# Slot table of a mixture-of-experts layer summed by TensorE in PSUM, in place of ten scatters through memory

## The reference, cut to what matters

```
g_p, g_idx = top_k(softmax(x @ router_group_w + b), 1)          # 1 of 4 groups
e_p, e_idx = top_k(softmax(logits of the 8 experts there), 2)   # 2 of 8 experts
weights = g_p * e_p / sum(e_p)
hid = silu(x @ w_gate[e]) * (x @ w_up[e])                       # e: 1024 -> 256
out = sum over the 2 experts of weights[e] * (hid @ w_down[e])
```

## Time and profile before

| what | value |
|---|---|
| time, median of 3 runs (range) | 1311.78 us (1309.76 to 1312.71) |
| profiled execution: its time, its span | 1309.53 us, 1307.7 us |
| PE busy, DVE busy, ACT busy, POOL busy | 70%, 47%, 22%, 7% of the span |
| granted TensorE clock, mean | 0.789 of 2.4 GHz |
| HBM read, written | 181.74 MB, 19.36 MB |

### The profile page before, as it was taken

One profiled execution on the slowest core, in us unless ns is written; L12 is line 12 of the kernel. 1 busy time (PEld: TensorE's weight loads), 2 busy tenths in 40 slices (PEclk: granted clock), 3 DMA queues, 4 the chain that ended last, 5 costly groups with the idle time before them and its releaser, 6 DMA issues. The chain is left out here.

```text
span 1307.7 us, 15405 instructions
## 1 busy us (share of the span) xinstructions
PE 919.8 (70%) x5907; PEld 578.9 (44%) x5907; DVE 615.1 (47%) x1286; ACT 294.1 (22%) x499; POOL 89.3 (7%) x71
## 2 busy tenths in 40 slices
PE   1699988989368786776867659983047899697710
PEld 1365555666255665665756324452012344242300
DVE  2317999355568676786742432335601111010124
ACT  2230000323525244273211540101000111010102
POOL 0000000010010010100100000001311111111031
PEclk9889999989675575755756779985568999798965
DMA  9835511200110011101140730110359999989543
GB/s 334 291 153 210 196 55 57 75 9 17 17 26 9 10 25 17 26 1 18 25 164 3 276 163 33 49 49 19 147 232 381 394 421 419 377 340 398 193 156 145
DMA packets 72967, 193.72 MB, mean 148 GB/s; under 512 B 42629, under 2 KB 43023, under 8 KB 58687
## 3 DMA queue, kind: packets, MB, share of 16 engines
q1 hardware_dynamic: 64272, 174.05, 35.8%
q0 software_dynamic: 5840, 10.63, 2.1%
q10 hardware_dynamic: 2783, 8.06, 1.7%
HBM read 181.74 MB, written 19.36 MB: 154 GB/s over the span
## 5 line engine op out<-in xcount | busy, mean ns | idle before, releaser
L521 PE MATMUL bank<-arena 128*128 128x320 f32 x704 | 200.8, 445 | 14.3 <-DVE arena L413 6.1
L521 PEld LDWEIGHTS bank<-arena 128*128 128x128 f32 x704 | 135.3, 194 | 81.5 <-issue 30.0
L1998 PE MATMUL bank<-arena 128*64 128x512 f32 (+2 forms) x528 | 131.0, 668 | 34.7 <-DMA arena<-in_expert_w_up 33.6
L921 DVE SCALAR_TENSOR_TENSOR arena<-arena 128x655 f32<-128x655 f32 x116 | 104.7, 902 | 4.6 <-DVE arena L921 0.2
L1998 PEld LDWEIGHTS bank<-arena 128*64 128x64 f32 (+2 forms) x528 | 45.7, 151 | 118.3 <-issue 116.9
L1466 PE MATMUL bank<-arena 128*128 128x512 f32 x160 | 78.6, 655 | 11.6 <-issue 11.6
L2079 DVE TENSOR_TENSOR arena<-arena,bank 128x256 f32<-128x256 f32 x17 | 7.2, 422 | 161.6 <-ACT arena L2053 161.6
L2020 PE MATMUL bank<-arena 128*64 128x512 f32 (+2 forms) x264 | 62.4, 599 | 9.9 <-DVE arena L2082 9.9
L883 ACT ACTIVATE arena<-bank 64x128 f32<-64x128 f32 (+1 forms) x68 | 19.9, 292 | 170.7 <-PE bank L1256 169.4
L1466 PEld LDWEIGHTS bank<-arena 128*128 128x128 f32 x160 | 33.4, 211 | 54.2 <-issue 54.2
L1984 PE MATMUL bank<-arena 128*128 128x128 f32 x136 | 19.7, 290 | 52.9 <-DMA arena<-tokens_for_experts,arena 52.9
(11 more groups left out here) (309 smaller groups left out, 1440.9 us busy)
## 6 DMA issues: line engine op xcount, KB each, us to landing
arena<-in_expert_w_gate SPq DMA_DIRECT2D x33, 1024.0 KB, 14.4
arena<-in_expert_w_up SPq DMA_DIRECT2D x33, 1024.0 KB, 17.2
arena<-in_expert_w_down SPq DMA_DIRECT2D x33, 1024.0 KB, 18.3
arena<-in_ada_w SPq DMA_DIRECT2D x12, 2048.0 KB, 10.2
arena<-in_w_in SPq DMA_DIRECT2D x22, 512.0 KB, 3.7
arena<-expert_rows SPq DMA_DIRECT2D x10, 512.0 KB, 8.4
arena<-in_x_sample SPq DMA_DIRECT2D x8, 512.0 KB, 7.7
arena<-in_w_out SPq DMA_DIRECT2D x1, 4096.0 KB, 14.7
```

The lines of the kernel that those rows point to most:

```text
L521: mm = nc.tensor.matmul(psum[4 + 2 * (n % 2) + half][:, 0:HALF], wring[:, n % NWIN, k], hT[:, k, half * HALF:(half + 1) * HALF], start=(k ...
L921: chain(nc.vector.scalar_tensor_tensor(acc, src, w, acc, ALU.mult, ALU.add))
L1998: mm = nc.tensor.matmul(psum[2 + n % 2][r, :], xeT[:, n % 2, c, r], gu[:, :, c, :], start=(c == 0), stop=(c == KD - 1))
```

## The change

The table is made in PSUM. For each of the 10 columns DVE writes a one-hot of the row's lane (128 x 128, `lane_hot`) and a one-hot of its tile times its two values (128 x 74, `tile_val`), and PE sums the 10 products; DVE then turns the sums into token, output row and gate value in `tab`. The table is still stored to `slots`, behind everything, since the overflow rounds read a column of it there. The blank table, the 10 scatters and the read are gone.

The ranking is done with one expert per partition: PE brings the 32 counts to rows and columns of 32 partitions, DVE compares and looks the rank's first tile, lane offset and size up in a constant (`rank_rows`), and PE spreads three values per expert over all partitions and gives the experts in order of rank. `s_ids` is announced as soon as that is there. POOL's memset of `xe` no longer has a table write ahead of it. Constants for the one-hots (`late`, 261 columns) are loaded with the modulation rows. SP's load 4 waits for `s_ovst` alone.

```
@@ dve_route
-            chain(nc.vector.memset(initt[:, :, 2:4], 0.0))
-            chain.announce(nc.vector.memset(initt[:, :, 0:2].bitcast(I32), MISS), s_tinit0, 1)
...
+            for src, own, dst in ((iot, t32, krow), (lane0, kc, kcol)):
+                chain(nc.vector.tensor_scalar(own, src, float(FIXED_EXPERTS[1]), 2.0, ALU.is_equal, ALU.mult))
+                chain(nc.vector.scalar_tensor_tensor(own, src, float(FIXED_EXPERTS[0]), own, ALU.is_equal, ALU.add))
+                chain(nc.vector.scalar_tensor_tensor(dst, own, -65536.0, src, ALU.mult, ALU.subtract))
+            e_ = slice(0, 32)
+            dve.wait_ge(s_cnt, 1)
+            chain(nc.vector.scalar_tensor_tensor(key[e_], psum[4][e_, 0:32], 32.0, krow[e_], ALU.mult, ALU.add))
+            chain(nc.vector.scalar_tensor_tensor(kc[e_], psum[4][e_, 32:33], 32.0, kcol[e_], ALU.mult, ALU.add))
+            chain(nc.vector.tensor_scalar(gt[e_], key[e_], kc[e_], None, ALU.is_gt))
+            chain(nc.vector.tensor_reduce(rank[e_], gt[e_], AX_X, ALU.add))
+            chain(nc.vector.tensor_scalar(onehot[e_], iot[e_], rank[e_], None, ALU.is_equal))
...
-            chain(nc.vector.tensor_tensor(cmp_, key.unsqueeze(1).broadcast_to(w3), key.unsqueeze(2).broadcast_to(w3),
-                                          ALU.is_gt))
-            chain(nc.vector.tensor_reduce(rank, cmp_, AX_X, ALU.add))
...
+            dve.wait_ge(s_vec, 1)
+            chain.announce(nc.vector.tensor_copy(eid[0:1].bitcast(I32), psum[5][0:1, 96:128]), s_ids, 1)
+            chain(nc.vector.tensor_copy(vrow, psum[5][:, 0:96].rearrange("p (v e) -> p v e", e=32)))
...
+            chain(nc.vector.tensor_tensor(tile_hot, const("slot_row").unsqueeze(1).broadcast_to(st),
+                                          flat_tile.unsqueeze(2).broadcast_to(st), ALU.is_equal))
+            chain(nc.vector.tensor_tensor(tile_val, tile_hot.unsqueeze(2).broadcast_to(sv),
+                                          vals.unsqueeze(3).broadcast_to(sv), ALU.mult))
+            chain.announce(nc.vector.tensor_tensor(lane_hot, const("lane_row").unsqueeze(1).broadcast_to(sl),
+                                                   flat_lane.unsqueeze(2).broadcast_to(sl), ALU.is_equal), s_pos, 1)
+            dve.wait_ge(s_tabsum, 1)
...
+            chain.announce(nc.vector.tensor_copy(tab[:, :, 2], psum[7][:, NSLOT:2 * NSLOT]), s_tab, 1)
@@ pe_route
+            for i in range(TILES):
+                nc.tensor.matmul(psum[4][0:32, 0:32], ones[:, 0:32], both[:, i], start=(i == 0), stop=(i == TILES - 1))
+            for i in range(TILES):
+                mm = nc.tensor.matmul(psum[4][0:32, 32:34], both[:, i], ones[:, 0:2], start=(i == 0), stop=(i == TILES - 1))
+            mm.then_inc(s_cnt, 1)
...
+            pe.wait_ge(s_pos, 1)
+            for n in range(NLANE):
+                mm = nc.tensor.matmul(psum[7][:, 0:2 * NSLOT], lane_hot[:, n], tile_val[:, n].rearrange("p v s -> p (v s)"),
+                                      start=(n == 0), stop=(n == NLANE - 1))
+            mm.then_inc(s_tabsum, 1)
@@ pool_route, act_table
-            pool.wait_ge(s_tinit0, 1)
-            pool.dma_start(slots.rearrange("(p a) b -> p a b", p=P), initt.bitcast(I32)).then_inc(s_tinit, 16)
...
-            for n in range(NLANE):
-                pool.indirect_dma_start(out=slots, out_offset=At(ap=sloti[:, n:n + 1].bitcast(U32), axis=0),
-                                        in_=ent[:, n, :].bitcast(I32), in_offset=None).then_inc(s_scat, 16)
...
-            act.dma_start(tab.bitcast(I32), slots.rearrange("(p a) b -> p a b", p=P)).then_inc(s_tab, 16)
+            act.dma_start(slots.rearrange("(p a) b -> p a b", p=P), tab.bitcast(I32)).then_inc(s_slotst, 16)
```

More of the change, by code:

```diff
@@ L50 @@
 NPAR = _at
+CAP = P // 2
+NHOT, NPAIR, NQUAD = 6, 6, 3
+NTILE = NHOT + 1 + NPAIR + NQUAD + 1
+NOV = 20
+NSLOT = NTILE + NOV
+SECOND, COLD, FIXED = NHOT + NPAIR, NHOT + 2 * NPAIR, NEXP - 2
+FIXED_EXPERTS = (0, 16)
+MISS = 1 << 20
+ROWS = [(NTILE - 1, (FIXED, FIXED + 1))]
+_taken = {"S": 0, "P": 0, "Q": 0}
+for _kind in "PQPSSPSPSSQHPQP":
+    if _kind == "H":
+        ROWS += [(0, (0,)), (1, (0,))]
+        continue
+    _m = _taken[_kind]
+    _taken[_kind] += 1
+    ROWS.append({"S": (2 + _m, (1 + _m,)), "P": (NHOT + 1 + _m, (NHOT + _m, SECOND + _m)),
+                 "Q": (NHOT + 1 + NPAIR + _m, tuple(COLD + _m + NQUAD * j for j in range(4)))}[_kind])
 CONSTS = [("ident", 128), ("headones", 128), ("ones", 128), ("gmask", 128), ("scanmask", 512),
-          ("before", 128), ("expiota", 32), ("lanes", 8), ("ovi", 24), ("sel", 2)]
+          ("before", 128), ("expiota", 32), ("lanes", 8), ("ovi", 24), ("sel", 2),
+          ("lane_row", 128), ("slot_row", NSLOT), ("rank_rows", 96)]
 COFF = {}
@@ L120, in build @@
         keep = Region(0)
-        cst = keep.take(NCONST)
+        cst = keep.take(NKEEP)
         par = keep.take(NPAR)
@@ L1322, in build @@
         eid = regp.take(32)
+        late = regp.take(NCONST - NKEEP)
         regs = Region(ebuf[NB - 1], ebuf[1])
@@ L1713, in dve_route @@
             chain(nc.vector.reciprocal(t2, t2))
[L1714 to L1720, removed]
+            chain(nc.vector.tensor_copy(vals[:, 0:TILES, 1], t2))
+            chain(nc.vector.tensor_tensor(vals[:, TILES:NLANE, 1], t2, t3, ALU.mult))
+            chain(nc.vector.memset(tab, 0.0))
             dve.wait_ge(s_rank, 1)
@@ L1778, in dve_route @@
-            for k in range(2):
-                chain(nc.vector.tensor_copy(e2[:, k * TILES:(k + 1) * TILES, 0], tok))
-                ins_ = nc.vector.tensor_scalar(e2[:, k * TILES:(k + 1) * TILES, 1], tok, float(k * T), None, ALU.add)
-                if k == 0:
-                    chain(ins_)
-            chain.announce(ins_, s_ent, 1)
-            chain(nc.vector.tensor_tensor(cmp_, rank.unsqueeze(1).broadcast_to(w3), iot.unsqueeze(2).broadcast_to(w3),
-                                          ALU.is_equal))
@@ L1787, in dve_route @@
-            chain(nc.vector.tensor_tensor(cmp_, cmp_, iot.unsqueeze(1).broadcast_to(w3), ALU.mult))
-            chain(nc.vector.tensor_reduce(key, cmp_, AX_X, ALU.add))
-            chain.announce(nc.vector.tensor_copy(eid.bitcast(I32), key), s_ids, 1)
+            chain(nc.vector.tensor_scalar(big, sec, float(P + 1), None, ALU.is_ge))
+            chain(nc.vector.scalar_tensor_tensor(tl, dd, float(-P), isov, ALU.is_ge, ALU.subtract))
+            chain(nc.vector.tensor_tensor(tl, tl, big, ALU.mult))
@@ new lines, in dve_route @@
+            chain(nc.vector.scalar_tensor_tensor(dest, psum[7][:, 0:NSLOT], 1.0, blank, ALU.subtract, ALU.add))
+            chain(nc.vector.tensor_scalar(blank, dest, float(T), float(-T), ALU.is_ge, ALU.mult))
+            chain(nc.vector.tensor_tensor(blank, blank, dest, ALU.add))
+            ti = tab.bitcast(I32)
+            chain(nc.vector.tensor_copy(ti[:, :, 0], blank))
+            chain(nc.vector.tensor_copy(ti[:, :, 1], dest))
+            chain.announce(nc.vector.tensor_copy(tab[:, :, 2], psum[7][:, NSLOT:2 * NSLOT]), s_tab, 1)
@@ L2223, in _constants @@
     c["ovi"] = np.tile(np.arange(24), (P, 1))
+    c["lane_row"] = np.tile(np.arange(P), (P, 1))
+    c["slot_row"] = np.tile(np.arange(NSLOT), (P, 1))
+    first = np.zeros((3, NEXP))
+    for tile, ranks in reversed(ROWS):
+        rows = P // len(ranks)
+        for j, k in enumerate(ranks):
+            first[0, k], first[2, k] = tile, rows * sum(k in r for _, r in ROWS)
+            first[1, k] = first[2, k] + rows * j
+    c["rank_rows"] = np.tile(first.reshape(1, 96), (P, 1))
     c["sel"] = (i[:, None] % 32 == np.arange(2)[None]) * 1.0
```

132 lines of the change are left out of this document (61 added, 71 removed).

## The result

The changed kernel takes 1289.57 us (median of 4 runs, 1286.99 to 1292.88) against 1310.77 us (4 runs) of the kernel before: ratio 0.9849, 95% interval 0.9819 to 0.9878, that is 16 to 24 us less: under 2%, but clear of the scatter. Two later sets of the same kernel gave 0.9842 and 0.9838.

A forecast was written before the change was run, and what follows sets the result against it. Taken as bound by the slot table and the DVE chain ahead of PE's first tile. Steps summed to 23.8 us gained: 1309.5 to 1285.7 for the profiled execution, 1288.0 against the median of 1311.78; range 1285 to 1296.

The forecast's parts named there:

- What bounds: Slot table and the DVE chain ahead of it delay PE's first tile; the weight stream starts with that tile.
- Start of the routing: POOL's memset holds the first DVE tensor_scalar until 902.65; experts picked at 909.2 instead of 908.9, plus 0.3 us.
- DVE to the marks: DVE from expert pick to one-hot marks: 11.7 us removed, 10.25 added, net minus 1.5; marks ready at 928.7.
- Waits for PE inside it: Ten small counting matmuls take 1.2 us plus 0.2, hidden under six key steps to 0.1; at the bound DVE waits 3.2.
- The table: Ten PE matmuls, 20 records, take 4.4 us plus 0.2; DVE's reading 1.5; table at 934.8 instead of 952.7.
- The gather: First gather of token rows runs alone, taking 3.7 us instead of 9.59; bounds 2.6 and 9.6.
- Together: All steps up to PE's first tile: it starts at 939.4 instead of 963.23, a gain of 23.8 us.
- Downstream: Behind the first tile everything moves whole; load 5 comes 12 us behind it; load 4, if late, is late by 1 us.
- A contended gather: Rival: first gather still takes 9.6 us, or PE is at its upper bounds; gain 17.9, 1293.9 us; chance 0.15.
- The stream did not follow load 4: Rival claimed the weight stream follows load 4, not PE, so only 12.9 us are kept: 1299 us; chance 0.06.
- the case with more gain: Rival: late memset (1.3), gather 2.6 us (1.1), tile 0 at 2.4 GHz (7.3 for 8.81 us); gain 27.7, 1284; chance 0.05.
- TensorE was not held at 1.2 GHz over whole tiles: Slower rival claimed PE stays at 1.2 GHz after its early start, 11 us more per tile; four give 1332; chance 0.03.

The follow-up runs named there:

- memset_early: The changed kernel with POOL's memset of the gather buffers no longer waiting for the last router matmul; mean 1287.4 us over two sets, ratios 0.9844 and 0.9833.
- pe_busy: The changed kernel plus unused 512-column matmuls on PE, 14 behind the spread of the ranks and 6 behind the table's sum; mean 1284.3 us, ratio 0.9804.
- both: The changed kernel with POOL's memset ahead of the routing and unused PE matmuls, 14 ahead of the table, 8 behind; ratio 0.9811 in its first set.
- both2: Second set of the kernel called both, measured beside the changed kernel; median 1280.8 us, ratio 0.9765 to the kernel before.
- loads_held: The changed kernel with SP waiting for the slot table ahead of loads 2 and 3; mean 1299.4 us, ratio 0.9926 to the kernel before.
- rank_only: The changed kernel with its new ranking, but the slot table made through memory as before; mean 1302.5 us, ratio 0.9954 to the kernel before.
- before_load4_late: The kernel before, with SP's load 4 waiting until the first gather has landed; mean 1305.3 us, ratio 0.9978 to the kernel before.

## Why the prediction was right

Counted from the router's end (898.95 in the trace of before), step by step:

- **What bounds.** Right: the stretch to the first tile shrank by 22.6 us, and the kernel by 20 to 21. That everything behind the first tile "moves whole" was a little too much: 1 to 2 us of it are waited out at the weights.
- **Start of the routing.** Right, with its mechanism. The experts are picked 10.2 us behind the router, as forecast; the tensor_scalar was held for 3.23 us, and memset_early shows that the memset is what held it.
- **DVE to the marks.** 30.2 us measured, 29.75 forecast. The ranking steps took 1.9 us where I gave 1.8, and the memset of `tab` (0.18 us) was not in the sum.
- **Waits for PE inside it.** Right: the count matmuls took 0.74 and 0.67 us for ten records each, and L1727 started at 908.97, right behind the last key step.
- **The table.** 4.54 us for 20 records, where I had 4.4 plus 0.2. The nearer row decided rightly. In pe_busy the same records take 2.45 us at clock 1.00, 0.12 us each. The Trainium skill, "TensorE: Matmul & The Clock Gate", section LDWEIGHTS, gives columns over 1.2, an estimate of 107 ns for 128 columns: that would have given about half of what was measured, and is near what a record takes here at 2.4 GHz. DVE's reading took 1.6 instead of 1.5.
- **The gather.** The mechanism was right and shown from both sides (4.24 and 4.26 us without loads beside it, 9.51 to 10.22 with them); the size was 0.5 us short. The row that I took was one transfer; here three more gathers are issued from 1.4 us on, and whether they are the reason is not shown.
- **Together.** The first tile 41.7 us behind the router instead of 40.45: a gain of 22.6 where I had 23.8. That the absolute times agree better (938.99 and 939.4) is only because this execution reached the router's end 1.6 us sooner.
- **The time.** 1288.0 against 1289.57 (1288.9 over 16 runs) is closer than the working deserves. The base of the sum, 1311.78, was the median of three runs; the kernel before has a mean of 1309.3 over 50. From there 23.8 us less would be 1285.5, and what was gained is 20.4: the gain was forecast 3.4 us too high, 1.2 of it at the first tile and the rest behind it, and the high base made up for most of it. Nor do three or four runs of this kernel tell 2.6 us from no change: the interval of the result is 4 us to either side.
- **Downstream.** Load 5 came 12.8 us behind the first tile, not 12: gate and up of tile 0 took 9.66 us, not 8.81. Over the other eleven traces (all but those of both and both2) it is 8.81 to 10.10, and the trace of before was the fastest of them, so its row was not a typical one. I gave a load 4 that comes late 1 us; by loads_held its cost is what is left of it in flight, there some 5 us at tile 2.
- **The rivals.** A contended gather is real, but needs the loads to be held. The stream did not follow load 4, which moved by 12.2 us behind the router where the kernel gained 20 to 21. The third part of the case with more gain (clock) did not come by itself, and is worth 2.4 to 3.0 us in gate and up of tile 0 when PE is kept at work (7.09 against 9.66 to 10.10, and 9.45 and 9.84 with the memset early). TensorE was not held at 1.2 GHz over whole tiles: in the trace of the changed kernel the granted clock was 0.95 over 947 to 949 us and 1.00 from there to the end of the tile, so it rose in the middle of gate and up.

What the prediction did not see is how much of the old cost was collision: by rank_only 5 to 6 us of the 22.8 between entries and table were loads 2 and 3 beside the scatters and the read, and by before_load4_late 5.3 us of the gather were load 4. Added up, about half of what the first tile gained is thus a matter of when the weights are moved (early loads 2 and 3 need the new ranking, though); for the other half the path through memory has to go. The two were measured each by itself: a kernel with the early ranking and load 4 held, but the table still through memory, was not run.

## What to carry to other kernels

A small transfer on the path takes its own time only if nothing large is in flight: before replacing it, see what the queues were given just ahead of it, since one wait on SP may give a part of it (here a quarter of the step at the first tile, and 3.3 of 21 us at the end). Price a chain of small steps by a fit through the rows of the same engine, and a new matmul by the row with its weight width at the clock that PE will have after the wait in front of it. When PE waits for something short, see whether the wait ends at the slower clock, and what the work behind it takes then.

## What the runs showed of the hardware

- A DVE tensor_scalar that meets a running POOL memset is held until the memset ends: 2.57 and 3.23 us for what takes 0.18 without it. Instructions with two tensor inputs beside the memset were not held (0.32 us), nor was a reduction of 20 elements in the same trace (0.17 us at 900.88). The Trainium skill, "GPSIMD Engine Reference", section 1 Specifications, names VectorE instructions in a 2-port mode and those with two SBUF inputs as contending; for the second kind these traces show no hold, and the mode of an instruction stands in no trace.
- In pe_busy TensorE's granted clock was 1.00 in every stretch from 920 to 938 us, in which PE was kept at work up to 935.7, and 0.52 from 938 to 942, behind a wait of 1.97 us; in the kernel called both, where PE waited only 1.02 us for ACT, it was 1.00 through gate and up of the first tile (stretches from 916 to 943 us), and so in both2 from 925 to 940. That is one trace with the wait and two without.
- At the lower clock a record with 32-wide weights took 0.06 to 0.07 us, one with 128-wide weights and 74 columns 0.23.
- The last scatter of a slot table (128 rows of four 4-byte values, 2 KB) landed in 2.10 us with the queues nearly empty (DMA share 0.03) and in 6.02 to 6.06 us beside 6 MB of loads. Two of POOL's ten issues took 1.4 to 1.5 us instead of 0.97, at the time when SP issued loads 2 and 3; that SP's issues are the reason is not shown.
